# Hybrid encoder block on 8 cores: 46 of 145 weight units without write-back in the first tile, copied later by cast transfers in device memory, and a second pair of score banks in that tile

## The reference

```
u    = rmsnorm(h)
proj = u @ w_in                # 6656 columns: q, f, i, out-gate, pool, two merge gates
o    = hgrn2(q, f, i)          # gated linear recurrence, 8 heads of 128 x 128, chunkwise
ya   = (rmsnorm_per_head(o) * sigmoid(og)) @ w_br_hgrn
yb   = pool_mixer(xp) @ w_br_pool     # trailing means over 2, 4, 8, 16 tokens, per-group map
h    = h + (sigmoid(ga) * ya + sigmoid(gb) * yb) @ w_out
u    = rmsnorm(h)
h    = h + (silu(u @ w_ffn_gate) * (u @ w_ffn_up)) @ w_ffn_down      # width 2816
out  = rmsnorm(h)[:, 16:]
```

## Time and profile before

| | us |
|---|---|
| median of the runs | 2167.08 |
| the runs | 2166.81, 2477.38, 2167.08 |
| the profiled execution | 2170.29 |
| its span, slowest core (core 5) | 2168.7 |
| spans of the 8 cores | 2158.5 to 2168.7 |

### The profile page before, as it was taken

One profiled execution on the slowest core, in us unless ns is written; L12 is line 12 of the kernel. 1 busy time (PEld: TensorE's weight loads), 2 busy tenths in 40 slices (PEclk: granted clock), 3 DMA queues, 4 the chain that ended last, 5 costly groups with the idle time before them and its releaser, 6 DMA issues.

```text
span 2168.7 us, 38075 instructions; the slowest of 8 cores (2158.5 to 2168.7 us)
## 1 busy us (share of the span) xinstructions
PE 2088.9 (96%) x11476; PEld 1106.8 (51%) x11476; DVE 1001.8 (46%) x1756; ACT 1007.0 (46%) x1492; POOL 574.0 (26%) x671
## 2 busy tenths in 40 slices
PE   6777998999999999999999999999999999999997
PEld 3432554555555555555555555555555555554447
DVE  4644453447534742474246523662357235732223
ACT  4832763258415742464247623662358324731111
POOL 3121120001105251423243143314332414223300
PEclk9988999999999999999999999999999999999999
DMA  9999999887565666557555755575557555565577
GB/s 202 211 198 249 217 223 238 228 213 221 147 183 154 186 190 177 158 156 225 170 151 170 223 162 159 168 222 162 166 164 199 180 173 158 165 175 174 169 197 191
DMA packets 232789, 405.24 MB, mean 187 GB/s; under 512 B 24208, under 2 KB 66704, under 8 KB 232592
## 3 DMA queue, kind: packets, MB, share of 16 engines
q1 hardware_dynamic: 210080, 364.62, 57.6%
q0 software_dynamic: 20880, 36.32, 11.7%
q10 hardware_dynamic: 1632, 1.88, 0.4%
HBM read 385.94 MB, written 53.08 MB: 202 GB/s over the span
## 4 chain that ended last, share of the span: by engine, by line
PE 84%; DMA 12%; SPq 1%; issue 1%; DVE 1%; ACT 1%; POOL 0%; DVEq 0%; POOLq 0%; ACTq 0%
PE psa L496 75%; DMA wsc<-wr 6%; DMA wr<-wpk 5%; PE psa L661 5%; DMA wr<-wsc 1%; PE psa L782 1%; SPq L364 1%; PE psa L796 1%; PE psa L815 1%; PE psa L816 1%; PE psa L831 0%; DMA fa<-xT 0%; PE psa L620 0%; PE psa L601 0%; DVE ba L630 0%
## 5 line engine op out<-in xcount | busy, mean ns | idle before, releaser
L496 PE MATMUL psa<-ba,wr 128*128 128x456 bf16 (+2 forms) x8960 | 1776.7, 354 | 19.8 <-DVE ba L546 6.6
L496 PEld LDWEIGHTS psa<-ba,wr 128*128 128x128 bf16 x8960 | 868.1, 98 | 830.2 <-issue 40.6
L906 DVE TENSOR_TENSOR ba<-psa,fa 128x456 bf16<-128x456 f32 (+1 forms) x198 | 124.5, 631 | 250.8 <-PE psa L496 213.0
L905 ACT ACTIVATE fa<-psa 128x456 f32<-128x456 f32 (+1 forms) x198 | 107.1, 551 | 217.1 <-PE psa L496 185.1
L589 POOL TENSOR_TENSOR fa<-fa 128x456 f32<-128x456 f32 (+1 forms) x160 | 158.0, 996 | 161.8 <-DMA fa<-xT 76.9
L773 POOL TENSOR_TENSOR ba<-fa 128x456 bf16<-128x456 f32 (+1 forms) x48 | 61.1, 1272 | 480.7 <-ACT fa L756 257.9
L363 POOL DMA_DIRECT2D wr<-wpk x145 | 76.8, 535 | 373.8 <-DMA wsc<-wr 180.6
L661 PE MATMUL psa<-wr,ba 128*114 128x512 bf16 (+1 forms) x576 | 136.6, 384 | 3.0 <-DMA wr<-wpk 3.0
L765 DVE TENSOR_TENSOR_SCAN fa<-ba,fa 128x456 f32<-128x456 bf16 (+1 forms) x72 | 83.4, 1159 | 120.1 <-ACT fa L763 120.0
L866 POOL TENSOR_TENSOR fa<-fa 128x456 bf16<-128x456 f32 (+1 forms) x48 | 55.3, 1152 | 289.2 <-DVE fa L863 289.2
L863 DVE SCALAR_TENSOR_TENSOR fa<-fa,psa 128x456 f32<-128x456 f32 (+1 forms) x72 | 45.3, 629 | 165.9 <-PE psa L496 165.9
(11 more groups left out here) (84 smaller groups left out, 1767.2 us busy)
## 6 DMA issues: line engine op xcount, KB each, us to landing
wr<-wsc SPq DMA_DIRECT2D x1040, 256.0 KB, 3.0
wr<-wpk POOLq DMA_DIRECT2D x128, 256.0 KB, 14.3
wsc<-wr SPq DMA_DIRECT2D x128, 256.0 KB, 18.3
wr<-wsc SPq DMA_DIRECT2D x72, 192.0 KB, 2.8
fa<-xT SPq DMA_DIRECT2D x6, 1824.0 KB, 13.9
outT<-fa SPq DMA_DIRECT2D x6, 1824.0 KB, 11.0
wr<-wsc SPq DMA_DIRECT2D x72, 128.0 KB, 2.3
fa<-xT SPq DMA_DIRECT2D x2, 1840.0 KB, 13.2
```

Source lines behind the costliest of these rows:

```text
L496: last = e.matmul(ps[bank][:, 0:c1 - c0], lhsT=sl[0].ap(i * 128, (i + 1) * 128), rhs=s_.ap(c0, c1), start=(start and i == 0), stop=(stop a ...
L905: yield act(lambda e: e.activation(out=sg.ap(0, nt), in_=ps[bg][:, 0:nt], func=AF.Silu), [PS(bg)], [sg.rg(0, nt)], tset="S", banks=[bg])
L906: yield dve(lambda e: e.tensor_tensor(out=ACT[fc].ap(0, nt), in0=ps[bu][:, 0:nt], in1=sg.ap(0, nt), op=ALU.mult), [PS(bu), sg.rg(0, nt)], ...
```

## The change

1. **Late units.** 46 of the 145 units are put into `RAWCAST`: 18 of heads, merge and output projection (`LATE_M`: WOG3 to WOG7, WGA0, WBP1, WGB2, WBH2, WGA3, WBP4, WGB5, WBH5, WGA6, WBP7, WO0, WO3, WO6) and 28 of the feed-forward part (`LATE_F`: WU6 to WU21, WD01, WD10, WD12, WD21, WD30, WD32, WD41, WD50, WD52, WD61, WD70, WD72). In tile 0 they are loaded raw as before but not written back. The 18 of `LATE_M` are loaded raw once more in tile 1.
2. **Casts.** Their place in `wsc` is filled by a transfer from `wpk` to `wsc` with a cast, both in device memory ("cast" in what follows), on POOL's queue. The first is issued beside the load of WD00 of tile 0 (`CAST_AT`), then one at each fourth load issued (`CAST_STEP`), those of SP included; and a reload of a late unit first brings in all casts up to its own. Each cast has its own semaphore, d0 to d45, for which the reload in tile 1 or 2 waits.
3. **A second pair of score banks.** The odd heads of tile 0 use banks 3 and 4 for scores and output, the even ones 6 and 7 as before. The matrix products have three banks in place of five until head 7 of tile 0 has passed.

```diff
+LATE_M = [u for u in range(24, FF0) if u % 3 == 0]
+LATE_F = [u for u in range(FF0 + 12, NU) if u % 2 == 0]
+RAWCAST = sorted(LATE_M + LATE_F, key=lambda u: 2.0 * u if u < FF0 else 3.2 * (u - FF0))
+CAST_AT = NU - 24
+CAST_STEP = 4
...
-        KA_, PN_, O_ = 6, 5, 6
-        NDENSE = 5
+        KA_, KA2, PN_ = 6, 3, 5
...
-        free_banks = {b: 0.0 for b in range(NDENSE)}
+        free_banks = {b: 0.0 for b in range(KA2)}
...
+        def cast_next():
+            k = castpos[0]
+            if k < len(RAWCAST):
+                castpos[0] += 1
+                u = RAWCAST[k]
+                n = WU[u][4] * WU[u][5]
+                P.emit("pool", lambda e: e.dma_start(out=wsc[u, :, 0:n], in_=wpk[u, :, 0:n]), w=[(("dr", u), 0, 1)], sem=f"d{k}", inc=16, dma=True, dur=0.54, xfer=XL)
...
+            if t == 0 and u == CAST_AT:
+                castpos[1] = 1
+            if castpos[1]:
+                castpos[1] += 1
+                if castpos[1] % CAST_STEP == 0:
+                    cast_next()
-            if t == 0:
+            if t == 0 or (t == 1 and u in LATE_M):
                 P.emit("pool", lambda e: e.dma_start(out=sbuf, in_=wpk[u, :, 0:n]), aft=early(), w=[sb.rg(0, n)], sem=f"v{slot}", inc=16, dma=True, dur=0.54, xfer=XL)
-                pend.append((slot, lambda: P.emit("sp", lambda e: e.dma_start(out=back, in_=sbuf), r=[sb.rg(0, n)], w=[(dk, 0, 1)], sem=f"b{slot}", inc=16,
-                                                  dma=True, dur=0.4, xfer=XB), nissue[0]))
-                if u == NU - 1:
+                if u not in RAWCAST:
+                    pend.append((slot, lambda: P.emit("sp", lambda e: e.dma_start(out=back, in_=sbuf), r=[sb.rg(0, n)], w=[(dk, 0, 1)], sem=f"b{slot}", inc=16,
+                                                      dma=True, dur=0.4, xfer=XB), nissue[0]))
+                if t == 0 and u == NU - 1:
                     flush()
             else:
+                while u in RAWCAST[castpos[0]:]:
+                    cast_next()
                 P.emit("sp", lambda e: e.dma_start(out=sbuf, in_=back), r=[(dk, 0, 1)], w=[sb.rg(0, n)], sem=f"w{slot}", inc=16, dma=True, dur=0.4, xfer=XS)
...
+            KB = KA2 if t == 0 and h % 2 else KA_
...
-            yield Lock("KA")
+            yield Lock(f"KA{KB}")
...
+            if (t, h) == (0, 7):
+                for b in (KA2, KA2 + 1):
+                    free_banks[b] = P.free["dve"]
```

More of the change, by code:

```diff
@@ L67 @@
 UIDX = {u[0]: i for i, u in enumerate(WU)}
+FF0 = UIDX["WG0"]
+LATE_M = [u for u in range(24, FF0) if u % 3 == 0]
[3 more added lines that the diff above has]
+CAST_STEP = 4
 XL, XB, XS = 1.6, 0.7, 0.75
@@ L268, in build_nc @@
         semnames += [f"{c}{i}" for c in "wvb" for i in range(NSLOT)]
+        semnames += [f"d{k}" for k in range(len(RAWCAST))]
         sems = {n: es.enter_context(nc.semaphore("s_" + n)) for n in semnames}
@@ L781, in ka_all @@
                     rhs = QI.t[0:128, QI.off:QI.off + 2 * step].rearrange("p (k s) -> p k s", k=2)[:, :, 0:128] if i else QI.ap(0, 256)
[L782 removed]
+                    last = e.matmul(ps[KB + i // 2][0:c, (i % 2) * 256:(i % 2) * 256 + 256], lhsT=s["Kb"].ap(i * c, (i + 1) * c), rhs=rhs, start=True, stop=True)
                 return last
[L784 removed]
+            yield Op("pe", ka_all, [s["Kb"].rg(0, nt), QI.rg()], [PS(KB), PS(KB + 1)], 0.5)
             yield dve(lambda e: e.tensor_tensor(out=ka.ap(0, 1024, p=c).rearrange("p (k c) -> p k c", k=4)[:, :, 0:128 + c],
[L786 removed]
+                                                in0=psa[0:c, KB * 512:KB * 512 + 1024].rearrange("p (k c) -> p k c", k=4)[:, :, 0:128 + c],
                                                 in1=CF.ap(C_MASK, C_MASK + 128 + c, p=c).rearrange("p (k c) -> p k c", k=1).to_broadcast([c, 4, 128 + c]), op=ALU.mult),
[L788 removed]
+                      [PS(KB), PS(KB + 1), CF.rg()], [ka.rg()], dur=1.2)
             if h == 0:
@@ L795, in p_all @@
                     vo = i * 1024 + h * 128
-                    last = e.matmul(ps[KA_ + 1][:, i * 128:(i + 1) * 128], lhsT=ka.ap(i * 256, i * 256 + 128, p=c), rhs=V.ap(vo, vo + 128, p=c), start=True, stop=True)
+                    last = e.matmul(ps[KB + 1][:, i * 128:(i + 1) * 128], lhsT=ka.ap(i * 256, i * 256 + 128, p=c), rhs=V.ap(vo, vo + 128, p=c), start=True, stop=True)
                 return last
-            yield Op("pe", p_all, [ka.rg(), V.rg()], [PS(KA_ + 1)], 0.5)
+            yield Op("pe", p_all, [ka.rg(), V.rg()], [PS(KB + 1)], 0.5)
             tb = [TCH.sub(0, 128), TCH.sub(128, 128), TCH.sub(256, 128), TST[h]]
@@ L814, in o_all @@
                     vo = i * 1024 + h * 128
-                    e.matmul(ps[O_][:, i * c:(i + 1) * c], lhsT=V.ap(vo, vo + 128, p=c), rhs=ka.ap(i * 256 + 128, i * 256 + 128 + c, p=c), start=True, stop=False)
-                    last = e.matmul(ps[O_][:, i * c:(i + 1) * c], lhsT=(s_in.ap() if i == 0 else st.ap((i - 1) * 128, i * 128)),
+                    e.matmul(ps[KB][:, i * c:(i + 1) * c], lhsT=V.ap(vo, vo + 128, p=c), rhs=ka.ap(i * 256 + 128, i * 256 + 128 + c, p=c), start=True, stop=False)
+                    last = e.matmul(ps[KB][:, i * c:(i + 1) * c], lhsT=(s_in.ap() if i == 0 else st.ap((i - 1) * 128, i * 128)),
                                     rhs=qq.ap(i * c, (i + 1) * c), start=False, stop=True)
                 return last
-            yield Op("pe", o_all, [V.rg(), qq.rg(0, nt), ka.rg(), s_in.rg(), st.rg()], [PS(O_)], 0.9)
+            yield Op("pe", o_all, [V.rg(), qq.rg(0, nt), ka.rg(), s_in.rg(), st.rg()], [PS(KB)], 0.9)
             if h >= 2:
                 yield Gate(("head", t, h - 2))
-            yield act(lambda e: e.activation(out=sq.ap(0, nt), in_=ps[O_][:, 0:nt], func=AF.Square), [PS(O_)], [sq.rg(0, nt)])
+            yield act(lambda e: e.activation(out=sq.ap(0, nt), in_=ps[KB][:, 0:nt], func=AF.Square), [PS(KB)], [sq.rg(0, nt)])
             yield Gate(("g", t, h))
-            yield dve(lambda e: e.scalar_tensor_tensor(out=osb.ap(0, nt), in0=thg.ap(0, nt), scalar=1.0, in1=ps[O_][:, 0:nt], op0=ALU.add, op1=ALU.mult),
-                      [thg.rg(0, nt), PS(O_)], [osb.rg(0, nt)])
-            yield Unlock("KA")
+            yield dve(lambda e: e.scalar_tensor_tensor(out=osb.ap(0, nt), in0=thg.ap(0, nt), scalar=1.0, in1=ps[KB][:, 0:nt], op0=ALU.add, op1=ALU.mult),
+                      [thg.rg(0, nt), PS(KB)], [osb.rg(0, nt)])
+            yield Unlock(f"KA{KB}")
             yield dve(lambda e: e.tensor_scalar(out=s_out.ap(), in0=TST[h].ap(), scalar1=s["eb"].ap(nt - 1, nt), scalar2=None, op0=ALU.mult),
```

5 lines of the change are left out of this document (3 added, 2 removed).

## The result

The changed kernel took 2210.86 us in the median of its runs against 2167.01 us; the ratio is 1.0188, with a 95% interval from 1.0116 to 1.0261. Two later measurements of the same program gave 1.0142 (1.0082 to 1.0202) and 1.0200 (1.0137 to 1.0263). The forecast was 2169 us, within 2151 to 2194; the change costs 30 to 45 us. The profiled execution took 2202.73 us, 32.4 us over that of before. (Each kernel had an execution in which the granted clock of one die was low, and that lifts the medians; ratios leave such runs out.)

What follows compares the result with a forecast made beforehand. The prediction took full DMA to bound PE before 368 us and PE's own rate after. Profiled 2170.29 us - 10.1 - 8.6 + 21.0 of new stalls gave 2172.6 us, about 2169 us as median, range 2151 to 2194.

Steps and rivals of the forecast that it cites:

- the first view: Whole kernel: PE's losses lie at the start; only idle time before 368 us, or new idle time behind it, can change.
- The waits near 350 us: Around 350 us: PE's waits for reloads behind write-backs, and its slower matmuls there, go; 8.6 us gained.
- no release: Rival, before 200 us: slots or PE, not DMA work, hold the loads, so dropped write-backs free nothing; 2179 us, chance 0.05.
- cheap casts: Rival, behind 350 us: a cast costs what a raw load does, 1.75 us; stalls 10.3 us, total 2158 us, chance 0.28.
- The gain before 360 us: Tile 0 and around 350 us: PE comes 18.7 us earlier, 10.1 us from dropped write-backs and 8.6 us near 350 us.
- so I take all 10.1 us: Before 200 us: 13.5 units without write-back, 0.75 us each, bring the last output projection load and PE 10.1 us forward.
- Merge 1: From merge 1 to V of tile 2: transfers outlast PE's work, giving stalls of 10.8 and 4.8 us.
- Behind it: After V of tile 2: stalls of 1.8 us up to the last down projection and 3.6 us at nine casts.
- Nine casts then go out at once: After tile 1's last down projection: casts and 15 reloads exceed 28 us of PE work; 3.6 us of stall.
- 35 us of casts fit over some 70 us of PE: nothing: Last sixteen casts, behind norm work ending at 551.8 us: reloads take 0.51 of the DMA, so no stall.
- bursts that starve the reloads: Rival, rows of nine and sixteen casts: turns by packet shut reloads out, 13 and 12 us more; 2194 us, chance 0.20.
- Too few dense banks: Rival, tile 0: three projection banks freed late by ACT make heads end later; 2177 us if 10 us later, chance 0.07.

Runs made afterwards that it cites:

- The banks alone: The kernel before with only the second pair of score banks in tile 0, every unit written back and no cast: 2168.59 us against 2168.19, ratio 1.001.
- The run with a late start: The changed kernel with its first cast 15 units later and casts behind the last raw load waiting for landings: ratio 1.0201 to the kernel before.
- The run with holds: The changed kernel with each of 27 casts behind tile 0's last raw load waiting until the load issued with it landed: 2187.95 us, ratio 1.0087.
- The extra casts: The kernel before plus 24 unneeded casts, twelve in tile 4 (16 rows), twelve in tile 6 (128 rows): 2212.36 us queued, 2179.74 us spread.

## Why the prediction was wrong

**What held.** The loss lies where the first view put it, and only before 640 us. The waits near 350 us went with the write-backs, so "no release" fell. The casts' price was booked at 2.3 us and measured at 2.33 us of DMA time a unit, with 2.16 us (76.0% of 37 us for 3.42 MB) as the lowest in a row of casts; the "cheap casts" rival (1.75 us) fell with it. The estimate of 2.2 us from the Trainium skill (HBM Reference, "Specifications (TRN2)", its row "Effective per core") is near it too. The banks alone gave nothing (1.001), and the DMA stayed full to beyond 500 us.

**The gain before 360 us: 12.1 us, not 18.7.** The step "so I take all 10.1 us" was mis-sized. I read the heads on one core, the one that ended last, where the last scores start at 123.00 us and the merge at 130.76 us. On the other seven the merge starts at 135.98 to 138.42 us; on core 6 the last scores start at 129.53 us and the merge at 137.29 us. From there merge and projection need 60 us of PE (138.20 to 198.6 us in the changed kernel, where 224 matmuls run without a wait), not the 56 us that I had. In the changed kernel the merge starts at 132.68 to 140.53 us, and on every core the last group starts 58 to 60 us behind it. So PE, and no longer the loads, sets that point, and the gain there differs by core: 1.6 us on core 1 (200.03 to 198.39), 5.8 us on core 6, 10.0 us on core 4 (203.58 to 193.56). My own condition, that PE must not be late itself, was met on the core that I looked at and not on the others. On core 5 too the merge starts at 138.50 us in the changed kernel, 7.7 us later than before; why heads end early or late on a core is open. The rest of the 12.1 us came by 356 us, where PE no longer waits.

**Merge 1: 26.9 us lost between the marks, not 15.6.** I had 74.1 us of transfers for the stretch up to V of tile 2; it took 83 us. The engines gave a share of 0.997 there (60.8% and 38.9%), not the 1.045 that I called full, which is 3.6 us. Queue 1 cost 38.9% of 83 us for 7.96 MB, 4.06 us per MB where I had taken 3.53 for reloads and 2.98 for write-backs, some 4.5 us more. Queue 0 took 60.8% of 83 us, 50.5 us, where I had booked 50. That agreement is luck: its 7.12 MB are 27 units and I had counted 24, so a count too low met a price too high (1.86 us a unit in the mean of casts and raw loads there). So here the sum was the right kind of sum, with two of its rates too good and a count too low; the other 2.4 us are PE's own time, which I put at 58.5 us and which was 56.1 between the marks of before. The run with a late start shows that all of this loss came from the casts. And PE waited there for reloads, 18.9 us of its 20.6, and not mostly for raw loads as I had it. Whether turns by packet play a part in merge 1, beside the sum of the work, no run separates.

**Behind it: 18.9 us, not 5.4.** The failed step is "Nine casts then go out at once (8 units, 18.4 us) beside 15 reloads (13.2 us) in 28 us of PE: 3.6 us" and "35 us of casts fit over some 70 us of PE: nothing". Both added up work as if what PE needs first were served first. The queues' packets were served nearly one for one, and with a row of casts in one of them the reloads had 11 to 21% of the DMA. The run with holds takes nothing away but the queueing, and both losses go. So the rival "bursts that starve the reloads" was the true case, with its place and its mechanism. I gave it 0.20 and priced it at 2194 us. Its size was not right: it put 25 us on top of the 5.4, 30.4 us behind merge 1, where 18.9 were measured. That its total is near the measured time comes of this error and the two above, which lie the other way. The Trainium skill (DMA: Bandwidth & Descriptors, "Queues, rings and completion order") has each engine go round the queues by packet. The counts, 299 to 296, 893 to 937 and 1340 to 1338, agree. I let that case turn on how a cast is cut. The extra casts bear that out for the share: queue 1 got 30.5% beside small packets and 11.0% beside large ones. For the kernel's time they don't: the changed kernel with smaller rows ran no faster (1.0128 against 1.0142). Why is open; that queue 1 had fewer packets served than queue 0 there (1207 to 1492) says that at times it had none ready.

**Too few dense banks** fell as a cause of loss. That the casts' waits in SP's order played a part in the changed kernel isn't seen: SP shows no wait for a cast there. It shows 78.9 us of them once the casts start later.

## What to carry to other kernels

A transfer that nobody waits for isn't free because there is room: in a queue that takes turns with the one that feeds PE, twelve in a row cost 7.5 us where the DMA share had been 0.69 (1200 to 1280 us), and the same twelve, each tied to the landing of a load, cost nothing. A plan's spacing of transfers holds on the chip only if a wait enforces it; with none, an idle issuing engine sends them in one row (nine in 4.44 us, sixteen in 7.90 us). Work taken out of the front of a kernel has to be put back where PE has no need of the same engines, early enough that nobody waits for it: with 46 units no such place was found, with 18 it was, and that gave 0.2%.

## What the runs showed of the hardware

A cast from float32 to bf16 within device memory costs 2.33 us of full DMA for a unit of 128 x 1024, 1.27 times a raw load into a slot (1.83 us). In the other rows of casts it came to 2.16 us and, cut as 128 rows of 1024 in place of 16 of 8192, to 2.23 us (69.6% of 30 us for 2.45 MB) and 2.34 us (62.9% of 37 us for 2.61 MB): the cut makes no clear difference to the price. Beside casts queue 1, mostly reloads, costs more, 4.06 us per MB against 3.53. And two queues with 299 and 296 packets served in 25 us had 87.7% and 11.0% of the engines' time, with 1340 and 1338 packets in 30 us 69.6% and 30.5%: what came out even in these stretches is the count of packets, not time or bytes, and large packets take the time from the other queue. Where a queue has at times none ready, the counts part too (1492 to 1207).
